# Two expert layers: the order of puts, picks and gate-and-up products in the block loop of a one-core transformer kernel

## The chip, the core and the metric

The kernel runs on one core of one Trainium2 chip. The core has a matrix engine (PE, or TensorE, with its weight loads shown apart as PEld), a vector engine (DVE), a scalar engine (ACT), a general engine (POOL), and a sync engine (SP) whose queue here issues nearly all DMA transfers. Each engine runs its own instruction list in order and waits on semaphores. The metric is the device time of one execution in microseconds. Before the change it is 2860.58 us, the median of 3 runs (2859.57 to 2863.24).

## The reference, cut to what matters

Two model blocks run one after the other on 256 tokens of width 1024. The second has two layers, each of which ends in a routed expert layer: a router picks 2 of 32 experts for each token, tokens are gathered by expert into blocks, and each block goes through its expert.

```python
def expert_block(args):
    x_blk, e = args
    hidden = jax.nn.silu(x_blk @ w_gate[e]) * (x_blk @ w_up[e])
    return hidden @ w_down[e]

yb = lax.map(expert_block, (xb, blk_e)).reshape(cap, d)
out = jnp.zeros((n_tok + 1, d), t.dtype).at[buf_tok].add(yb * buf_w[:, None].astype(yb.dtype))
```

Each expert has three float32 matrices, gate and up (1024 x 512) and down (512 x 1024), 2 MB each. So a layer reads 32 times 6 MB. The first expert layer has 512 tokens (the 256 and a context of 256), the second 256.

## The kernel before, in words

All work is written out by hand for each engine: `pe_program`, `act_program`, `dve_program`, `pool_program` and `sp_program` build one instruction list each, and semaphores tie them together. The order in a list is the order in the code. No planner moves anything.

An expert layer works in blocks of 32 token rows (`BL`). How many blocks an expert has is known only at run time, so for each of the 32 experts every engine has a loop `Fori(first_block(e), first_block(e + 1))` over the block number `g`. `first_block` (L2492) loads a register from memory, and each loop needs two. Since a block has only 32 rows, the matrix engine computes four column groups side by side (`q` in 0 to 3).

The steps of a block of the first expert layer (the "picked" layer, `pe_experts_picked`, L2741) are:

- **picks**: a 0/1 matrix times the token rows gathers the block's rows into PSUM (`pe_pick_rows`, L2736, 16 products, which the profile counts as 32 matmuls since float32 takes two passes). ACT copies them out (`xe`, L2793), PE transposes them (`pe_turn_picked`, L3232), and DVE copies them to `xeT` (L2803). DVE makes the pick matrix (`dve_places`, L2724 to L2730). Picks are done one block ahead: block `g` picks the rows of `g + 1`.
- **gate and up** products (L2761, 64 products, 128 matmuls) of `xeT` with the expert's first two matrices.
- **hidden**: ACT applies silu (L2791), DVE multiplies with the up half (L2821), PE transposes (L2768), DVE copies out (`hT`, L2824).
- **down** products (L2776, 16 products, 32 matmuls), copied out by ACT (L2796) and stored to memory by POOL (L2843).

In the code before, PE does gate and up of `g`, then the picks of `g + 1`, then the transpose of hidden, the transposes of the picked rows, and the down products. ACT does silu, then the copy of the picked rows, then the copy of the result.

The second expert layer (the "rows" layer, `pe_experts_rows`, L3245) differs at both ends. After the picks' transposes DVE applies gain and shift in two operations (`dve_turned`, L3352 and L3354). The result is not stored but added into PSUM by **puts** (`pe_put`, L3240): a transposed placement matrix `putT` times the block's result `yb`, in two halves around the picks. DVE makes `yb` (L3378), the pick matrix (`dve_picks`, L3322 to L3328) and the put matrix (`dve_puts`, L3337 to L3343) after the down products of each block, PE transposes the put matrix (L3276), and ACT copies it out (L3313). Puts are done one block late: block `g` puts the result of `g - 1`. The order on PE is gate and up, puts and picks, the transposes, and down.

The expert matrices come by SP's queue (L2361) into memory slots: nine in the picked layer, ten in the rows layer. When an expert's last block is done, a small matmul (L2779, L3291) signals `moe_ended`, and SP issues the transfers that reuse its slots. So the matrices of expert `e + 3` are asked for when expert `e` ends. In front of each expert's loop PE waits for the gate and up slots (L2753, L2754; L3256, L3257). The wait for the down slot is inside the loop.

Of the kernel before, what the change touches and what calls it, by code (L numbers as in the profile page):

```python
# [9 lines left out]
ACT = mybir.ActivationFunctionType  # L10
# [5 lines left out]
KT = D // P  # L16
# [2724 lines left out]
def pe_experts_picked(k, m):  # L2741
    pe, s, ps, l, BL, W, F = k.nc.tensor, k.s, k.ps, m.l, m.BL, m.W, m.F
    pe.wait_ge(*s["r_dve"].at(l, "based"))
    pe.wait_ge(*m.step("picks", 0, 2, 3))
    pe.wait_ge(*s["xs_out"].at(*HALVES[-1]))
    pe_pick_rows(k, m)
    pe.wait_ge(*m.step("x_out", 0, 1, 1))
    pe_turn_picked(k, m)
    for e in range(NE):
        sl = expert_slots(e)  # L2750
        wg, wu = (k.wslots[sl[i]].rearrange("p (k f) -> p k f", k=KT) for i in range(2))
        wd = k.wslots[sl[2]].rearrange("p (k f) -> p k f", k=4)
        pe.wait_ge(*s[f"slot{sl[0]}"].at("expert", l, e))  # L2753
        pe.wait_ge(*s[f"slot{sl[1]}"].at("expert", l, e))  # L2754
        with pe.Fori(first_block(k, m, e, ENG.PE), first_block(k, m, e + 1, ENG.PE)) as g:
            pe.wait_ge(*m.step("x_ready", g, 1, 1))
            pe.wait_ge(*m.step("hidden", g, 0, 1))
            for wv, a in ((wg, 0), (wu, F)):
                for t in range(KT):
                    for q in range(4):  # L2760
                        last = pe.matmul(ps[BL * q:BL * q + BL, 0, a:a + F], m.xeT[:, t, :], wv[:, t, F * q:F * q + F], start=(t == 0), stop=(t == KT - 1),  # L2761
                                         tile_position=(0, BL * q), skip_group_check=True)
            last.then_inc(m.n["gated"].sem, 1)
            pe.wait_ge(*m.step("picks", g, 5, 3))
            pe_pick_rows(k, m)
            pe.wait_ge(*m.step("hidden", g, 1, 1))
            pe.wait_ge(*m.step("h_ready", g, 0, 1))
            pe.transpose(ps[:, 2, 0:P], m.hb, k.c["ident"]).then_inc(m.n["h_turned"].sem, 1)  # L2768
            pe.wait_ge(*m.step("x_out", g, 2, 1))
            pe_turn_picked(k, m)  # L2770
            pe.wait_ge(*s[f"slot{sl[2]}"].at("expert", l, e))
            pe.wait_ge(*m.step("h_ready", g, 1, 1))
            pe.wait_ge(*m.step("y_ready", g, 0, 1))
            for f in range(4):
                for q in range(4):
                    last = pe.matmul(ps[BL * q:BL * q + BL, 3, 0:W], m.hT[:, f, :], wd[:, f, W * q:W * q + W], start=(f == 0), stop=(f == 3),  # L2776
                                     tile_position=(0, BL * q), skip_group_check=True)
            last.then_inc(m.n["down"].sem, 1)
        pe.matmul(ps[0:32, 0, 511:512], k.c["ident"][:, 0:32], k.c["ident"][:, 0:1], start=True, stop=True, skip_group_check=True).then_inc(*s["moe_ended"].up(l, "expert", e))  # L2779


def act_experts_picked(k, m):
    act, s, ps, l, BL, W = k.nc.scalar, k.s, k.ps, m.l, m.BL, m.W
    act.wait_ge(*s["r_dve"].at(l, "based"))
    act.wait_ge(*m.step("x_picked", 0, 1, 1))
    act.activation(m.xe, ps[:, 1, 0:256], ACT.Copy).then_inc(m.n["x_out"].sem, 1)
    for e in range(NE):
        with act.Fori(first_block(k, m, e, ENG.Activation), first_block(k, m, e + 1, ENG.Activation)) as g:
            act.wait_ge(*m.step("gated", g, 1, 1))
            act.wait_ge(*m.step("hidden", g, 0, 1))  # L2790
            act.activation(m.sil, ps[:, 0, 0:m.F], ACT.Silu).then_inc(m.n["silu"].sem, 1)  # L2791
            act.wait_ge(*m.step("x_picked", g, 2, 1))
            act.activation(m.xe, ps[:, 1, 0:256], ACT.Copy).then_inc(m.n["x_out"].sem, 1)  # L2793
            act.wait_ge(*m.step("down", g, 1, 1))
            act.wait_ge(*m.step("y_gone", g, 0, 1))
            act.activation(m.yring[:, bass.ds((g & 3) * W, W)], ps[:, 3, 0:W], ACT.Copy).then_inc(m.n["y_ready"].sem, 1)  # L2796
    act.activation(m.unread[:, 0:1], k.eps, ACT.Copy).then_inc(m.n["y_ready"].sem, 1)
# [447 lines left out]
def pe_experts_rows(k, m):  # L3245
    pe, s, ps, l, BL, W, F = k.nc.tensor, k.s, k.ps, m.l, m.BL, m.W, m.F
    pe.wait_ge(*s["r_dve"].at(l, "based"))
    pe.wait_ge(*m.step("picks", 0, 2, 3))
    pe_pick(k, m)
    pe.wait_ge(*m.step("x_out", 0, 1, 1))  # L3250
    pe_turn_picked(k, m)
    for e in range(NE):
        sl = row_slots(e)
        wg, wu = (k.wslots[sl[i]].rearrange("p (k f) -> p k f", k=KT) for i in range(2))
        wd = k.wslots[sl[2]].rearrange("p (k f) -> p k f", k=4)
        pe.wait_ge(*s[f"slot{sl[0]}"].at("expert", l, e))  # L3256
        pe.wait_ge(*s[f"slot{sl[1]}"].at("expert", l, e))  # L3257
        with pe.Fori(first_block(k, m, e, ENG.PE), first_block(k, m, e + 1, ENG.PE)) as g:
            pe.wait_ge(*m.step("x_ready", g, 2, 2))
            pe.wait_ge(*m.step("hidden", g, 0, 1))  # L3260
            for wv, a in ((wg, 0), (wu, F)):
                for t in range(KT):
                    for q in range(4):
                        last = pe.matmul(ps[BL * q:BL * q + BL, 0, a:a + F], m.xeT[:, t, :], wv[:, t, F * q:F * q + F], start=(t == 0), stop=(t == KT - 1),  # L3264
                                         tile_position=(0, BL * q), skip_group_check=True)
            last.then_inc(m.n["gated"].sem, 1)
            pe.wait_ge(*m.step("puts_out", g, 0, 1))
            pe.wait_ge(*m.step("y_ready", g, 0, 1))
            pe_put(k, m, 0).then_inc(m.n["half_put"].sem, 1)
            pe.wait_ge(*m.step("picks", g, 5, 3))  # L3270
            pe_pick(k, m)
            pe.wait_ge(*m.step("half_put", g, 1, 1))
            pe_put(k, m, 1)
            pe.wait_ge(*m.step("puts", g, 2, 3))
            for t in range(2):
                last = pe.transpose(ps[:, 3, 256 + t * P:256 + (t + 1) * P], m.put[:, t, :], k.c["ident"])  # L3276
            last.then_inc(m.n["puts_turned"].sem, 1)
            pe.wait_ge(*m.step("x_out", g, 2, 1))
            pe_turn_picked(k, m)
            pe.wait_ge(*m.step("hidden", g, 1, 1))  # L3280
            pe.wait_ge(*m.step("h_ready", g, 0, 1))
            pe.transpose(ps[:, 2, 0:P], m.hb, k.c["ident"]).then_inc(m.n["h_turned"].sem, 1)
            pe.wait_ge(*s[f"slot{sl[2]}"].at("expert", l, e))
            pe.wait_ge(*m.step("h_ready", g, 1, 1))
            pe.wait_ge(*m.step("puts_out", g, 1, 1))
            for f in range(4):
                for q in range(4):
                    last = pe.matmul(ps[BL * q:BL * q + BL, 3, 0:W], m.hT[:, f, :], wd[:, f, W * q:W * q + W], start=(f == 0), stop=(f == 3),  # L3288
                                     tile_position=(0, BL * q), skip_group_check=True)
            last.then_inc(m.n["down"].sem, 1)  # L3290
        pe.matmul(ps[0:32, 0, 511:512], k.c["ident"][:, 0:32], k.c["ident"][:, 0:1], start=True, stop=True, skip_group_check=True).then_inc(*s["moe_ended"].up(l, "expert", e))  # L3291
    total = first_block(k, m, NE, ENG.PE)
    pe.wait_ge(*m.step("puts_out", total, 0, 1))
    pe.wait_ge(*m.step("y_ready", total, 0, 1))
    pe_put(k, m, 0, stop=True).then_inc(m.n["half_put"].sem, 1)
    pe.wait_ge(*m.step("half_put", total, 1, 1))
    pe_put(k, m, 1, stop=True).then_inc(*s["acc_done"].up())


def act_experts_rows(k, m):  # L3300
# [3 lines left out]
    act.activation(m.xe, ps[:, 1, 0:256], ACT.Copy).then_inc(m.n["x_out"].sem, 1)  # L3304
    for e in range(NE):
        with act.Fori(first_block(k, m, e, ENG.Activation), first_block(k, m, e + 1, ENG.Activation)) as g:
            act.wait_ge(*m.step("gated", g, 1, 1))
            act.wait_ge(*m.step("hidden", g, 0, 1))
            act.activation(m.sil, ps[:, 0, 0:m.F], ACT.Silu).then_inc(m.n["silu"].sem, 1)  # L3309
            act.wait_ge(*m.step("x_picked", g, 2, 1))  # L3310
            act.activation(m.xe, ps[:, 1, 0:256], ACT.Copy).then_inc(m.n["x_out"].sem, 1)
            act.wait_ge(*m.step("puts_turned", g, 1, 1))
            act.activation(m.putT.rearrange("p t c -> p (t c)"), ps[:, 3, 256:512], ACT.Copy).then_inc(m.n["puts_out"].sem, 1)  # L3313


def dve_picks(k, m, g, wait=True):
# [309 lines left out]
```

## Time and profile before

| | |
|---|---|
| median of 3 runs | 2860.58 us |
| time of the profiled execution | 2861.28 us |
| its span, first to last instruction | 2860.1 us |
| busy: PE, PEld, DVE, ACT, POOL | 89%, 63%, 41%, 21%, 6% of the span |
| picked expert layer, first gate product to last down product | 1647.15 to 2132.8 us, 47 blocks |
| rows expert layer, the same | 2394.86 to 2850.0 us, 32 blocks |
| DMA read over the span | 670.09 MB |

The profile is of one execution. It lists, for each instruction, engine, start and duration, what the engine waited for before it, and the transfers with their landing. PEclk is the granted clock of the matrix engine as a share of full speed. A DMA share of 1 means that all 16 DMA engines were busy. "issue" is idle time of an engine for which no releasing instruction is seen. The chain of waits is followed back from the last instruction, each step to what released it. In it a transfer named there is one that some engine waited for.

### The profile page before, as it was taken

Reading aid. Unit: us, or ns where it says so; the run is one execution under the profiler, and the core shown is the slowest. Engines: PE = TensorE matmul, PEld = TensorE weight load, DVE = VectorE, ACT = ScalarE, POOL = GpSimd, SP = SyncE. Lnnn points to the kernel's source line nnn. Section 1 sums busy time; section 2 is a strip of 40 time slices with the busy share of each in tenths; the row PEclk is TensorE's granted clock in tenths of the full one; section 3 lists DMA queues with packets and bytes.
Section 4 is the critical chain, followed back from the end, with each engine's and each line's share of the span. In section 5 each row is a group of like instructions: output and inputs, shape, how many; then the busy total and the mean of one; then the engine's idle time right before and its main releaser. Section 6 shows DMA issues by size and latency. Waiting matters only on the chain.

```text
span 2860.1 us, 57236 instructions
## 1 busy us (share of the span) xinstructions
PE 2549.3 (89%) x23736; PEld 1804.0 (63%) x23736; DVE 1186.8 (41%) x2765; ACT 586.7 (21%) x1394; POOL 176.8 (6%) x346
## 2 busy tenths in 40 slices
PE   8999999998999999999998989887758997877776
PEld 7857778666857778668445566665546465554444
DVE  6563455646563465653138211111104253333323
ACT  3212322113212322122036211110102251000001
POOL 0001000010001000010000122221210000000000
PEclk9999999999999999999999999998978999999998
DMA  8844566456744566544210299999995126999997
GB/s 282 236 164 129 176 216 220 160 180 217 234 154 130 180 222 221 206 144 175 81 59 3 105 365 402 396 411 421 418 366 190 59 93 244 419 420 419 419 420 302
DMA packets 271389, 690.37 MB, mean 241 GB/s; under 512 B 35984, under 2 KB 163775, under 8 KB 254783
## 3 DMA queue, kind: packets, MB, share of 16 engines
q1 hardware_dynamic: 259904, 675.42, 63.1%
q0 software_dynamic: 7552, 10.76, 1.1%
q8 instruction: 168, 2.75, 0.4%
q10 hardware_dynamic: 3710, 0.99, 0.2%
q14 instruction: 55, 0.44, 0.0%
HBM read 670.09 MB, written 17.04 MB: 240 GB/s over the span
## 4 chain that ended last, share of the span: by engine, by line
PE 73%; DMA 14%; DVE 7%; issue 3%; ACT 2%; SPq 1%; ACTq 0%; POOL 0%; POOLq 0%; DVEq 0%
PE ps L756 18%; DMA arena<-in_moe_w_up 13%; PE ps L843 9%; PE ps L2761 5%; PE ps L1886 5%; PE ps L3264 3%; PE ps L2736 2%; PE ps L1945 2%; PE ps L2776 2%; PE ps L1251 2%; PE ps L2516 2%; PE ps L3225 1%; PE ps L3288 1%; PE ps L889 1%; PE ps L3070 1%
## 5 line engine op out<-in xcount | busy, mean ns | idle before, releaser
L756 PE MATMUL ps<-arena 128*128 128x256 f32 x2464 | 552.4, 381 | 9.9 <-DVE arena L1045 6.5
L756 PEld LDWEIGHTS ps<-arena 128*128 128x128 f32 x2464 | 460.6, 189 | 92.0 <-issue 13.0
L996 DVE TENSOR_TENSOR arena<-arena 128x1024 f32<-128x1024 f32 x176 | 214.8, 1223 | 143.4 <-PE ps L756 75.3
L843 PE MATMUL ps<-arena 128*128 128x512 f32 x616 | 266.1, 592 | 0.0
L2761 PE MATMUL ps<-arena 128*32 128x128 f32 x6016 | 196.4, 290 | 63.5 <-issue 61.0
L2761 PEld LDWEIGHTS ps<-arena 128*32 128x32 f32 x6016 | 180.6, 117 | 75.0 <-issue 69.7
L3264 PE MATMUL ps<-arena 128*32 128x128 f32 x4096 | 141.9, 298 | 80.0 <-issue 78.1
L843 PEld LDWEIGHTS ps<-arena 128*128 128x128 f32 x616 | 115.8, 189 | 144.4 <-issue 124.7
L3264 PEld LDWEIGHTS ps<-arena 128*32 128x32 f32 x4096 | 128.5, 120 | 85.3 <-issue 84.3
L2821 DVE TENSOR_TENSOR arena<-arena,ps 128x128 f32<-128x128 f32 x47 | 13.5, 288 | 313.7 <-ACT arena L2791 313.7
L1886 PE MATMUL ps<-arena 128*128 128x256 f32 (+2 forms) x384 | 133.4, 524 | 0.0
L2736 PE MATMUL ps<-arena 128*32 128x256 f32 x1536 | 101.1, 394 | 11.5 <-issue 8.4
L2843 POOL DMA_DIRECT2D expert_out<-arena x200 | 100.3, 502 | 69.3 <-issue 30.7
L1886 PEld LDWEIGHTS ps<-arena 128*128 128x128 f32 (+1 forms) x384 | 64.0, 172 | 62.8 <-issue 58.6
L3288 PE MATMUL ps<-arena 128*32 128x256 f32 x1024 | 62.1, 381 | 35.7 <-DVE arena L3376 35.7
L2776 PE MATMUL ps<-arena 128*32 128x256 f32 x1504 | 92.1, 381 | 0.4 <-issue 0.3
L920 ACT ACTIVATE arena<-ps 128x256 f32<-128x256 f32 x132 | 50.7, 384 | 147.7 <-PE ps L756 146.7
L2736 PEld LDWEIGHTS ps<-arena 128*32 128x32 f32 x1536 | 56.1, 112 | 37.2 <-issue 12.8
L1251 PE MATMUL ps<-arena 128*128 128x256 f32 x352 | 77.4, 379 | 0.0
L3309 ACT ACTIVATE arena<-ps 128x128 f32<-128x128 f32 x32 | 8.9, 278 | 318.7 <-PE ps L3264 318.7
L3225 PE MATMUL ps<-arena 128*32 128x256 f32 x528 | 69.6, 637 | 5.2 <-DVE arena L2480 3.3
L1251 PEld LDWEIGHTS ps<-arena 128*128 128x128 f32 x352 | 66.2, 189 | 9.5
(507 smaller groups left out, 3402.9 us busy)
## 6 DMA issues: line engine op xcount, KB each, us to landing
arena<-in_moe_w_gate SPq DMA_DIRECT2D x64, 2048.0 KB, 26.2
arena<-in_moe_w_up SPq DMA_DIRECT2D x64, 2048.0 KB, 26.2
arena<-in_moe_w_down SPq DMA_DIRECT2D x64, 2048.0 KB, 30.9
arena<-in_mod_w SPq DMA_DIRECT2D x24, 2048.0 KB, 13.9
arena<-in_w_gate SPq DMA_DIRECT2D x44, 1024.0 KB, 5.5
arena<-in_w_up SPq DMA_DIRECT2D x44, 1024.0 KB, 8.6
arena<-in_w_down SPq DMA_DIRECT2D x44, 1024.0 KB, 5.0
arena<-in_w_in SPq DMA_DIRECT2D x12, 1024.0 KB, 5.5
```

The source lines that it names most:

```text
L756: last = pe.matmul(out, tokens[j][:, t, :], weights[t], start=(t == 0 and j in ("P1", "P5", "P6", "P7")), stop=(t == HK - 1), skip_group_c ...
L843: pe.matmul(ps[:, DN_BANK[j], :], rows[j], w, start=(p == 0), stop=(p == CHUNKS - 1), skip_group_check=True).then_inc(*dn.up(l, f, p, j))
L996: V.tensor_tensor(out, a, b, op).then_inc(*s["w_sum"].up(l, f, c, i))
L1251: last = pe.matmul(dst, w[:, t, j * P:(j + 1) * P], src[:, t, :], start=(t == 0), stop=(t == KT - 1), skip_group_check=True)
L1886: last = pe.matmul(k.ps[o:o + m, j % 4, 0:ntok], w[:, t, c0:c0 + m], k.h2[:, t, 0:ntok], start=(t == 0), stop=(t == KT - 1), tile_position ...
L2736: last = k.nc.tensor.matmul(k.ps[32 * q:32 * q + 32, 1, 0:256], m.pick[:, t, :], m.rows[:, t, 256 * q:256 * q + 256], start=(t == 0), stop ...
L2761: last = pe.matmul(ps[BL * q:BL * q + BL, 0, a:a + F], m.xeT[:, t, :], wv[:, t, F * q:F * q + F], start=(t == 0), stop=(t == KT - 1), tile ...
L2776: last = pe.matmul(ps[BL * q:BL * q + BL, 3, 0:W], m.hT[:, f, :], wd[:, f, W * q:W * q + W], start=(f == 0), stop=(f == 3), tile_position= ...
L2843: k.nc.gpsimd.dma_start(k.ybuf[bass.ds(b * BL, BL), W * q:W * q + W], m.yring[BL * q:BL * q + BL, bass.ds((b & 3) * W, W)]).then_inc(which ...
L3225: last = k.nc.tensor.matmul(k.ps[32 * q:32 * q + 32, bank, 0:256], m.pick[:, t, :], rows, start=(t == 0), stop=(t == 1), tile_position=(0, ...
L3264: last = pe.matmul(ps[BL * q:BL * q + BL, 0, a:a + F], m.xeT[:, t, :], wv[:, t, F * q:F * q + F], start=(t == 0), stop=(t == KT - 1), tile ...
L3288: last = pe.matmul(ps[BL * q:BL * q + BL, 3, 0:W], m.hT[:, f, :], wd[:, f, W * q:W * q + W], start=(f == 0), stop=(f == 3), tile_position= ...
```

## The change

In both layers work that belongs to neighbouring blocks is moved to the front of the loop, ahead of the gate and up products. In the picked layer this is the picks of the next block. In the rows layer it is the two halves of the puts of the last block, the picks of the next, and the transposes of the put matrix. The waits for the gate and up slots move from in front of the loop into it, right before the products that need them. ACT's list follows: the copies of picked rows (and of the turned put matrix) come before silu. DVE, POOL and SP have the same lists as before.

```diff
@@ pe_experts_picked
-        pe.wait_ge(*s[f"slot{sl[0]}"].at("expert", l, e))
-        pe.wait_ge(*s[f"slot{sl[1]}"].at("expert", l, e))
         with pe.Fori(first_block(k, m, e, ENG.PE), first_block(k, m, e + 1, ENG.PE)) as g:
             pe.wait_ge(*m.step("x_ready", g, 1, 1))
+            pe.wait_ge(*m.step("picks", g, 5, 3))
+            pe_pick_rows(k, m)
+            pe.wait_ge(*s[f"slot{sl[0]}"].at("expert", l, e))
+            pe.wait_ge(*s[f"slot{sl[1]}"].at("expert", l, e))
             pe.wait_ge(*m.step("hidden", g, 0, 1))
...
             last.then_inc(m.n["gated"].sem, 1)
-            pe.wait_ge(*m.step("picks", g, 5, 3))
-            pe_pick_rows(k, m)
             pe.wait_ge(*m.step("hidden", g, 1, 1))
@@ act_experts_picked
+            act.wait_ge(*m.step("x_picked", g, 2, 1))
+            act.activation(m.xe, ps[:, 1, 0:256], ACT.Copy).then_inc(m.n["x_out"].sem, 1)
             act.wait_ge(*m.step("gated", g, 1, 1))
             act.wait_ge(*m.step("hidden", g, 0, 1))
             act.activation(m.sil, ps[:, 0, 0:m.F], ACT.Silu).then_inc(m.n["silu"].sem, 1)
-            act.wait_ge(*m.step("x_picked", g, 2, 1))
-            act.activation(m.xe, ps[:, 1, 0:256], ACT.Copy).then_inc(m.n["x_out"].sem, 1)
@@ pe_experts_rows
-        pe.wait_ge(*s[f"slot{sl[0]}"].at("expert", l, e))
-        pe.wait_ge(*s[f"slot{sl[1]}"].at("expert", l, e))
         with pe.Fori(first_block(k, m, e, ENG.PE), first_block(k, m, e + 1, ENG.PE)) as g:
-            pe.wait_ge(*m.step("x_ready", g, 2, 2))
-            pe.wait_ge(*m.step("hidden", g, 0, 1))
-            for wv, a in ((wg, 0), (wu, F)):
...
-            last.then_inc(m.n["gated"].sem, 1)
             pe.wait_ge(*m.step("puts_out", g, 0, 1))
             pe.wait_ge(*m.step("y_ready", g, 0, 1))
             pe_put(k, m, 0).then_inc(m.n["half_put"].sem, 1)
+            pe.wait_ge(*m.step("x_ready", g, 2, 2))
             pe.wait_ge(*m.step("picks", g, 5, 3))
             pe_pick(k, m)
             pe.wait_ge(*m.step("half_put", g, 1, 1))
...
             last.then_inc(m.n["puts_turned"].sem, 1)
+            pe.wait_ge(*s[f"slot{sl[0]}"].at("expert", l, e))
+            pe.wait_ge(*s[f"slot{sl[1]}"].at("expert", l, e))
+            pe.wait_ge(*m.step("hidden", g, 0, 1))
+            for wv, a in ((wg, 0), (wu, F)):
...
+            last.then_inc(m.n["gated"].sem, 1)
```

On PE, one expert of the picked layer reads in the order before as follows (L2495 are the register loads of `first_block`, L2761 gate and up, L2736 picks, L2768 the transpose of hidden, L3232 those of the picked rows, L2776 down):

```order
L2495 TENSOR_LOAD arena [waits slot0,slot5]
L2497 ISA
L2495 TENSOR_LOAD arena
L2497 ISA
L2755 UNCONDITIONAL_BRANCH
L2755 ISA
L2757 REGISTER_ALU [waits picked_x_ready]
L2761 MATMUL ps<-arena 32x128 [waits picked_hidden]
L2761 MATMUL ps<-arena 32x128 x63
L2764 ISA
L2736 MATMUL ps<-arena 32x256 [waits picked_picks]
L2736 MATMUL ps<-arena 32x256 x15
```

The same place after the change (here L2763 is gate and up):

```order
L2495 TENSOR_LOAD arena
L2497 ISA
L2753 UNCONDITIONAL_BRANCH
L2753 ISA
L2755 ISA [waits picked_x_ready]
L2736 MATMUL ps<-arena 32x256 [waits picked_picks]
L2736 MATMUL ps<-arena 32x256 x15
L2759 REGISTER_ALU [waits slot0,slot5]
L2763 MATMUL ps<-arena 32x128 [waits picked_hidden]
L2763 MATMUL ps<-arena 32x128 x63
L2768 MATMUL ps<-arena 128x128 [waits picked_h_ready,picked_hidden]
```

The slot wait has moved from the register loads to the gate products, and between the gate and up products and the transpose that waits for `hidden` nothing is left.

In the rows layer the list of PE after the change reads as follows (L3240 puts, L3225 picks, L3267 the transposes of the put matrix, L3275 gate and up, L3282 the transpose of hidden, L3288 down):

```order
L3240 MATMUL ps<-arena 128x256 [waits rows_y_ready,rows_puts_out]
...
L3225 MATMUL ps<-arena 32x256 [waits rows_picks]
...
L3240 MATMUL ps<-arena 128x256 [waits rows_half_put]
...
L3267 MATMUL ps<-arena 128x128 [waits rows_puts]
L3267 MATMUL ps<-arena 128x128
L3275 MATMUL ps<-arena 32x128 [waits rows_hidden,slot7,slot5]
L3275 MATMUL ps<-arena 32x128 x63
L3278 REGISTER_ALU
L3232 MATMUL ps<-arena 128x128 [waits rows_x_out]
L3232 MATMUL ps<-arena 128x128
L3282 MATMUL ps<-arena 128x128 [waits rows_h_ready,rows_hidden]
L3288 MATMUL ps<-arena 32x256 [waits rows_puts_out,rows_h_ready,slot9]
```

Before, the rows from L3240 to L3267 (then L3276) stood between the gate and up products and L3232. Now they stand ahead of the products, and the loop begins with the wait for `y_ready` of the block before.

## Rows read from the trace of the kernel before

**Rows 1.** Windows view, picked layer's first half: busy us per engine, PEclk, DMA share, GB/s

```profile
1660.00:1872.00 212.00, 191.97 (x4566) 140.72 (x4561) 40.82 (x143) 24.45 (x71) 50.36 (x115) 0.98 0.99 400
```

**Rows 2.** Windows view, same columns, rows layer from 2520 us

```profile
2520.00:2838.00 318.00, 226.02 (x4185) 152.82 (x4180) 94.32 (x364) 21.97 (x63) 0.00 (x0) 0.93 1.01 416
```

**Rows 3.** Chain of waits, where it leaves PE in the picked layer: start, us, what

```profile
1907.74 25.16 DMA arena<-in_moe_w_up
```

**Rows 4.** Timeline of SP's queue: issues of expert 15's down, expert 16's gate

```profile
1855.46 0.43 SPq L2361 DMA_DIRECT2D arena<-in_moe_w_down  x1
1871.86 0.34 SPq L2361 DMA_DIRECT2D arena<-in_moe_w_gate  x1
```

**Rows 5.** DMA view of these two issues: count, KB, us from issue to landing

```profile
arena<-in_moe_w_down SPq DMA_DIRECT2D x1, 2048.0 KB, 18.5
...
arena<-in_moe_w_gate SPq DMA_DIRECT2D x1, 2048.0 KB, 9.0
```

**Rows 6.** Timeline, a block of the picked layer from its picks on: start, us, engine

```profile
1849.77 1.95 PE L2736 MATMUL ps<-arena 128*32 128x256 f32 x32
1850.10 0.28 ACT L2791 ACTIVATE arena<-ps 128x128 f32<-128x128 f32 x1 [3.02 <-PE ps L2761]
1850.50 0.29 DVE L2821 TENSOR_TENSOR arena<-arena,ps 128x128 f32<-128x128 f32 x1 [4.71 <-ACT arena L2791]
...
1851.65 0.33 PE L2768 MATMUL ps<-arena 128*128 128x128 f32 x1
...
1852.02 0.29 DVE L2824 COPY arena<-ps 128x128 f32<-128x128 f32 x1 [1.23 <-PE ps L2768]
...
1852.19 0.44 PE L3232 MATMUL ps<-arena 128*128 128x128 f32 x2 [0.21 <-ACT arena L2793]
...
1852.56 1.93 PE L2776 MATMUL ps<-arena 128*32 128x256 f32 x32
```

**Rows 7.** Lines view of PE, 1647 to 1872 us: busy, mean ns, idle before

```profile
L2768 PE MATMUL ps<-arena 128*128 128x128 f32 x25 | 8.3, 334 | 0.0
```

**Rows 8.** Waits view of PE, the same stretch: total us, times, longest

```profile
PE ps L2761 <- issue: 9.0, 7, 2.9
...
PE ps L2736 <- issue: 4.4, 3, 2.0
```

**Rows 9.** Timeline, one block of the rows layer, from down products to down products

```profile
2467.04 1.94 PE L3288 MATMUL ps<-arena 128*32 128x256 f32 x32 [1.11 <-DVE arena L3376]
...
2469.03 0.42 DVE L3378 TENSOR_TENSOR arena<-ps,arena 128x256 f32<-128x256 f32 x1 [2.09 <-PE ps L3288]
...
2469.10 3.70 PE L3264 MATMUL ps<-arena 128*32 128x128 f32 x128
...
2470.32 0.23 DVE L3327 TENSOR_TENSOR arena<-arena 128x64 f32<-128x64 f32 x1
...
2472.73 0.71 PE L3240 MATMUL ps<-arena 32*128 32x256 f32 x8
...
2473.34 0.29 DVE L3372 TENSOR_TENSOR arena<-arena,ps 128x128 f32<-128x128 f32 x1 [1.15 <-ACT arena L3309]
...
2473.38 2.03 PE L3225 MATMUL ps<-arena 128*32 128x256 f32 x16
...
2476.26 0.38 PE L3232 MATMUL ps<-arena 128*128 128x128 f32 x2
...
2476.68 0.42 DVE L3352 TENSOR_TENSOR arena<-ps,arena 128x256 f32<-128x256 f32 x1 [3.05 <-PE ps L3232]
...
2477.86 1.94 PE L3288 MATMUL ps<-arena 128*32 128x256 f32 x32 [1.11 <-DVE arena L3376]
```

**Rows 10.** Chain of waits, last expert of each layer, from its weights' landing

```profile
2120.34 1.42 issue
2121.76 6.46 PE ps L2761 x128
...
2837.88 1.31 issue
2839.20 3.75 PE ps L3264 x128
```

More of the change, by code:

```diff
@@ L3255, in pe_experts_rows @@
         wd = k.wslots[sl[2]].rearrange("p (k f) -> p k f", k=4)
-        pe.wait_ge(*s[f"slot{sl[0]}"].at("expert", l, e))
-        pe.wait_ge(*s[f"slot{sl[1]}"].at("expert", l, e))
         with pe.Fori(first_block(k, m, e, ENG.PE), first_block(k, m, e + 1, ENG.PE)) as g:
-            pe.wait_ge(*m.step("x_ready", g, 2, 2))
-            pe.wait_ge(*m.step("hidden", g, 0, 1))
-            for wv, a in ((wg, 0), (wu, F)):
[L3262 to L3265, printed above, removed]
-            last.then_inc(m.n["gated"].sem, 1)
             pe.wait_ge(*m.step("puts_out", g, 0, 1))
@@ L3277, in pe_experts_rows @@
             last.then_inc(m.n["puts_turned"].sem, 1)
+            pe.wait_ge(*s[f"slot{sl[0]}"].at("expert", l, e))
+            pe.wait_ge(*s[f"slot{sl[1]}"].at("expert", l, e))
+            pe.wait_ge(*m.step("hidden", g, 0, 1))
+            for wv, a in ((wg, 0), (wu, F)):
+                for t in range(KT):
+                    for q in range(4):
+                        last = pe.matmul(ps[BL * q:BL * q + BL, 0, a:a + F], m.xeT[:, t, :], wv[:, t, F * q:F * q + F], start=(t == 0), stop=(t == KT - 1),
+                                         tile_position=(0, BL * q), skip_group_check=True)
+            last.then_inc(m.n["gated"].sem, 1)
             pe.wait_ge(*m.step("x_out", g, 2, 1))
@@ L3306, in act_experts_rows @@
         with act.Fori(first_block(k, m, e, ENG.Activation), first_block(k, m, e + 1, ENG.Activation)) as g:
-            act.wait_ge(*m.step("gated", g, 1, 1))
-            act.wait_ge(*m.step("hidden", g, 0, 1))
-            act.activation(m.sil, ps[:, 0, 0:m.F], ACT.Silu).then_inc(m.n["silu"].sem, 1)
             act.wait_ge(*m.step("x_picked", g, 2, 1))
@@ L3313, in act_experts_rows @@
             act.activation(m.putT.rearrange("p t c -> p (t c)"), ps[:, 3, 256:512], ACT.Copy).then_inc(m.n["puts_out"].sem, 1)
+            act.wait_ge(*m.step("gated", g, 1, 1))
+            act.wait_ge(*m.step("hidden", g, 0, 1))
+            act.activation(m.sil, ps[:, 0, 0:m.F], ACT.Silu).then_inc(m.n["silu"].sem, 1)
 def dve_picks(k, m, g, wait=True):
```

## The prediction, made before the changed kernel ran

> **What bounds the kernel now.** I read the windows first, then the chain of waits, then SP's issues with their landings, then the timeline of single blocks. The windows alone would mislead. From 1660 to 1872 us the picked layer shows a DMA share of 0.99 at 400 GB/s beside 191.97 us of PE work in 212 [rows 1], so both look full. The chain decides: it stays on PE from the first block until it leaves for a weight transfer at 1907.74 us [rows 3]. From there to the end of the layer PE waits for weights. The rows layer is the same with a short PE part. From 2520 us on the share is 1.01 at 416 GB/s and PE has 226.02 us of work in 318 [rows 2].
>
> Then I ask whether the transfers run free of PE in the first part. They do not. Expert 15's down matrix, issued at 1855.46, lands 18.5 us later, at 1874.0. Expert 16's gate matrix is issued at 1871.86, when expert 13 ends, and lands 9.0 us later, at 1880.9 [rows 4, 5]. That is 6.9 us after the transfer ahead of it, although 2.1 MB take 5.0 us at 416 GB/s [rows 2]. So the queue ran dry by 1.9 us: only 2.1 us of work was left in it at the issue. Each microsecond by which PE ends expert 13 later is a microsecond by which this matrix lands later, and from about here on the transfers are the bound with no slack to give it back. PE's block time in the first part sets the end of the layer.
>
> **The picked layer, per block.** Call E the start of the picks, when the gate and up products have been handed over: 1849.77. Before, the down products start at 1852.56, E + 2.79 [rows 6]. Under the picks lie silu (E + 0.33) and the multiplication (E + 0.73 to E + 1.02), so hidden is ready long before the picks end, and that wait is free. In the new order nothing covers it. PE idles from E to about E + 1.10, transposes hidden, and the copy starts 0.37 us after the transpose as now (1851.65 to 1852.02): E + 1.47 to E + 1.76. With 0.1 for the release, down starts at E + 1.86. The two transposes of the picked rows (0.44) fit behind hidden's, since their copy by ACT was done under the gate products. The picks still cost PE's time, now in front. They take 1.88 from their start to the next transpose [rows 6]; in front of narrower products I take 1.8. So a block costs 1.8 + 1.86 = 3.66 where it cost 2.79: **+0.87 us**. The pick matrix doesn't hold this up, since DVE has made it during the down products.
>
> 25 blocks are done by the end of expert 13 [rows 7]: 25 x 0.87 = 21.8. The first block must also wait for its successor's pick matrix, made after `x_ready`: +0.6, an estimate from two short DVE operations. Together 22.4.
>
> Something may give way. In this stretch PE stood 9.0 + 4.4 = 13.4 us in ten spells called "issue", inside rows of matmuls that wait for no one [rows 8]. I read these as instruction supply that comes late. If the new idle time falls between the request and the stall, the supply catches up, by at most 0.87 a spell: 8.7 in all. Bounds are 0 (the idle time falls elsewhere) and 13.4 (all go). The nearest reading is half of 8.7: **-4.4**.
>
> The Trainium skill (Runtime: NRT & Kernel Launch, section Instruction fetch mechanics) says that the next page of instructions is fetched while the current one runs and that the cost of a page boundary is mostly hidden. The spells in the trace, 13.4 us, do not fit "mostly hidden". By the page there would be nothing to win back, and the layer would pay the whole 22.4.
>
> **The picked layer's tail.** For the last expert, time runs from the landing of its up matrix. After the landing come 1.42 us of issue [rows 10]. The register loads of the loop stand behind the slot wait before and ahead of it after, so I take 1.3 of it as saved. From E on the tail is 2.79 - 1.86 = 0.9 shorter. **-2.2.** This holds only at the end. The same saving at each earlier expert hastens nothing, since the transfers don't wait for it there.
>
> **The rows layer, per block.** With S the start of the down products (2467.04), a block takes 10.82 to the next (2477.86). Gate and up take 3.63 of it (2469.10 to 2472.73) and 5.13 lie from their end to the down products [rows 9]. After the change, counted from S: `yb` is made from 1.99 to 2.41 and the first put starts at 2.46. It takes 0.65. The pick matrix is written at 3.28 to 3.51, so the picks start at 3.56. Picks, second put and the transposes of puts take 2.88 (2473.38 to 2476.26), to 6.44. Gate and up end at 10.07. Then silu and the multiplication, whose start is 0.61 after E (2473.34 against 2472.73) and whose end is at 0.90. DVE next applies gain and shift, which I let start at E + 0.87, and from that start to the down products it is 1.18 (2476.68 to 2477.86): E + 2.05. Sum 12.12: **+1.3 us** a block.
>
> All 32 experts have one block here, and from 2520 us on transfers need 15.1 us an expert (6.29 MB at 416 GB/s) [rows 2]. 12.1 plus a spell of issue stays under it. So only the first two experts' delay reaches the transfers, about 0.9 (the first block has no `yb` to wait for) and 1.3: **+2.2**, bounds 0 and 4. The tail gains 1.2 of the 1.31 of issue [rows 10] and 5.13 - 2.05 = 3.1, **-4.3**. It would be less (1.5 less) if the last gate products ran at the slow clock, as those of the picked layer do (6.46 for 128 against 3.75) [rows 10].
>
> **The sum.** 22.4 - 4.4 - 2.2 + 2.2 - 4.3 = +13.7. The profiled execution took 2861.28, so 2875.0. It lies 0.7 above the median, and on the median the forecast is **2874.3 us**. What is not in it: DVE, POOL and SP keep their order, and ACT has much idle time (24.45 us of work in 212) [rows 1].
>
> **Rivals.** *The transfers hide it all.* If the queue never really ran dry, the 22.4 and 2.2 fall away and the tails remain: -6.5, 2854 us, faster. For it speaks the share of 0.99 [rows 1]. Against it the landing 6.9 us behind the last one, and 400 GB/s where 416 are to be had. It would need over 20 us of queued work at the release of expert 13, and there were 2.1. Chance 0.07.
>
> *The late instruction supply takes up the idle time.* All 13.4 us go: 22.4 - 13.4 - 2.2 + 2.2 - 4.3 = +4.7, 2865 us, about the size that can't be told from none. For it speaks that the spells are there at all; against it that one spell of 2.9 is longer than the 0.87 a block adds [rows 8]. Chance 0.10.
>
> *The clock.* An idle stretch of 1.1 us in each block, then 0.2, is new in the picked layer. If the granted clock fell to its 1.2 GHz level in part of the blocks, gate and up would cost 6.46 instead of about 3.6 in each [rows 10], with 25 blocks up to +70; in a quarter of them +18, 2892 us. Against it: rows-layer blocks now wait 1.11 us each ahead of their down products, and gate and up after them still take 3.70 [rows 9]. Chance 0.08. The Trainium skill (TensorE: Matmul & The Clock Gate, section A second HAM failure mode: psum-queue depth-cycling) tells of a kernel whose short idle times between groups made the clock oscillate. It speaks against this change, but the granted 0.98 of [rows 1] is with idle times too, if shorter ones. By that rule it would be this rival's 2892 and by the row the forecast.
>
> *The rows layer becomes PE-bound too*, with long issue spells or slow gate products on top of 12.1, past the 15.1 from which it decides. At half a microsecond over in 27 experts, +14, 2888 us. Chance 0.05.
>
> **Numbers.** The forecast has 0.70. 0.2% of this time is 5.7 us, which is about what a measurement can tell from no change. Faster: 0.07 for hidden transfers and 0.01 from the rest, 0.08. Within: most of the second rival, 0.08. Slower: 0.84. The range goes from the second rival, 2864, to beyond the forecast with nothing won back (2879) and part of the clock's case, 2886.
>
> **What would show it.** In the profile after: the gap from the end of gate and up to down in the picked layer is 1.9 and not 2.8, with 1.1 of idle before L2768 released by DVE. Blocks cycle in 8.9 us instead of 8.0. The chain leaves PE for a transfer some 18 us later than 1907.74, or later still. The landing of a gate matrix in the first part stays about 9 us after its issue. No issue spell follows the last weights. The rows layer keeps its length within 3 us. Wrong would be: the picked layer no longer than before (then the transfers were the bound), or gate and up of 5 us and more in its first part (then it was the clock).

## The result, and the profile after

The changed kernel took 2875.91 us, the median of 6 runs (2872.21 to 2881.22), against 2861.98 before in the same session (6 runs). The ratio is 1.0049, with a 95% interval of 1.0037 to 1.0061: about 14 us slower, which is past the 0.2% that can be told from no change. Forecast were 2874.3 us and slower. A second timing in another session gave 1.0047 (1.0030 to 1.0064). The ratio should be carried on and not the times, since the kernel before gave medians of 2864 to 2866 us in the later sessions.

The windows of the profile after, the answer to [rows 1, 2] (busy us per engine, PEclk, DMA share, GB/s):

```profile
1660.00:1890.00 230.00, 194.25 (x4788) 152.54 (x4781) 39.51 (x144) 25.46 (x73) 54.32 (x124) 0.99 0.94 375
2535.00:2850.00 315.00, 228.59 (x4221) 150.79 (x4221) 92.33 (x362) 21.91 (x63) 0.00 (x0) 0.96 1.01 419
```

In the first part of the picked layer the transfers now move 375 GB/s and not 400, at a share of 0.94 and not 0.99. The clock has not fallen. The rows layer is as full as it was. The DMA engines have lost time in one place, and it is the one where PE sets the pace.

The chain of waits leaves PE for a transfer here, where [rows 3] had 1907.74:

```profile
1959.65 35.04 DMA arena<-in_moe_w_up
```

It is 52 us later, more than the delay of the layer. The transfer named here was issued when expert 19 ended, the one before when expert 16 ended (1907.07), so the chain leaves PE three experts later. It isn't PE's first wait for weights: it had already stood 3.19 us for expert 20's up matrix, until 1964.25, which the chain does not pass.

SP's issue of expert 16's gate matrix and its landing, which answer to [rows 4, 5]:

```profile
1886.22 0.34 SPq L2361 DMA_DIRECT2D arena<-in_moe_w_gate  x1
```

```profile
arena<-in_moe_w_gate SPq DMA_DIRECT2D x1, 2048.0 KB, 8.9
```

From issue to landing it took 8.9 us, as before 9.0, so the queue ran dry again and the delay of the issue (14.4 us, of which 1.8 arose ahead of the layer) went straight into the landing.

A block of the picked layer, from its gate and up products on, the answer to [rows 6]. L2763 is gate and up, L2793 silu:

```profile
1870.08 3.68 PE L2763 MATMUL ps<-arena 128*32 128x128 f32 x128
...
1873.91 0.28 ACT L2793 ACTIVATE arena<-ps 128x128 f32<-128x128 f32 x1 [3.19 <-PE ps L2763]
1874.30 0.29 DVE L2821 TENSOR_TENSOR arena<-arena,ps 128x128 f32<-128x128 f32 x1 [6.86 <-ACT arena L2793]
...
1874.65 0.33 PE L2768 MATMUL ps<-arena 128*128 128x128 f32 x1 [0.88 <-DVE arena L2821]
...
1875.01 0.29 DVE L2824 COPY arena<-ps 128x128 f32<-128x128 f32 x1 [0.42 <-PE ps L2768]
...
1875.41 1.93 PE L2776 MATMUL ps<-arena 128*32 128x256 f32 x32 [0.21 <-issue]
...
1877.13 1.94 PE L2736 MATMUL ps<-arena 128*32 128x256 f32 x32
```

(The profile counts two matmuls for each float32 product, here x128 for 64; no run shows why.) The brackets show the new idle time: 0.88 us before the transpose of hidden, ended by the multiplication on DVE, and 0.21 before the down products. From these down products to the next it is 8.79 us (1875.41 to 1884.20), where it was 8.03. That holds inside an expert. Where the expert changes, an unhindered interval was 8.36 us and is now 8.97.

PE's waits from 1647 to 1895 us, the answer to [rows 8]:

```profile
PE ps L2768 <- DVE arena L2821: 21.9, 25, 0.9
PE ps L2763 <- issue: 10.3, 5, 3.1
PE ps L2776 <- issue: 5.8, 25, 0.7
...
PE ps L2736 <- issue: 0.8, 1, 0.8
```

25 blocks waited 21.9 us for the multiplication. The view ends 9 us after expert 13, and one spell of 2.3 us (at 1891.3) belongs to expert 14. Up to expert 13's end (1885.92) the spells of late instructions are 5 with 8.8 us (8.0 and 0.8), where there were 10 with 13.4. The 5.8 of L2776 is mostly the 0.21 of each block.

One block of the rows layer, the answer to [rows 9]. L3275 is gate and up, L3267 the transposes of the put matrix:

```profile
2486.09 1.94 PE L3288 MATMUL ps<-arena 128*32 128x256 f32 x32 [0.71 <-issue]
...
2488.65 0.71 PE L3240 MATMUL ps<-arena 32*128 32x256 f32 x8 [0.63 <-DVE arena L3378]
...
2489.65 2.03 PE L3225 MATMUL ps<-arena 128*32 128x256 f32 x16 [0.28 <-DVE arena L3327]
...
2492.62 3.71 PE L3275 MATMUL ps<-arena 128*32 128x128 f32 x128
...
2497.22 0.33 PE L3282 MATMUL ps<-arena 128*128 128x128 f32 x1 [0.52 <-DVE arena L3372]
```

The three waits forecast are there: for `yb`, for the pick matrix and for hidden. The first put starts 2.56 after the down products (forecast 2.46), the picks 3.56 (3.56), gate and up 6.53 (6.44). The block takes 12.17 us (2486.09 to the next down products at 2498.26), with 12.12 forecast.

Both tails, the answer to [rows 10], in the chain of waits:

```profile
2135.09 0.23 issue
2135.32 4.93 PE ps L2763 x112
2140.26 1.08 issue
...
2143.77 3.18 PE ps L2776 x32
```

```profile
2853.47 2.62 issue
2856.09 5.40 PE ps L3275 x128
...
2863.38 1.97 PE ps L3288 x32
```

Of the 1.42 us after the last landing 0.23 are left. But the down products at the picked layer's end take 3.18 us and not 1.91, and the gate products at the rows layer's end 5.40 and not 3.75: both ran in part at the 1.2 GHz level (granted clock 0.61 and 0.68 over them), the second after 2.62 us of idle PE.

### The profile page after: what moved, and what is told of

Read it like the earlier page. It is cut to its first block, busy times and chain, and to the rows that moved or that the text cites. A ratio compares the mean times of both kernels' runs of the same rounds, so it can differ in the third digit from the quotient of the medians.

```text
span 2875.5 us, 57251 instructions
## 1 busy us (share of the span) xinstructions
PE 2552.6 (89%) x23736; PEld 1812.6 (63%) x23736; DVE 1181.4 (41%) x2765; ACT 586.3 (20%) x1394; POOL 176.8 (6%) x346
## 4 chain that ended last, share of the span: by engine, by line
PE 73%; DMA 13%; DVE 7%; issue 3%; ACT 2%; SPq 2%; ACTq 0%; POOL 0%; DVEq 0%; POOLq 0%
PE ps L756 18%; PE ps L843 9%; DMA arena<-in_moe_w_down 7%; PE ps L2763 5%; PE ps L1886 5%; DMA arena<-in_moe_w_up 4%; PE ps L2776 3%; PE ps L1945 2%; PE ps L2736 2%; PE ps L1251 2%; PE ps L3275 2%; PE ps L2516 2%; SPq L2361 2%; PE ps L3288 1%; PE ps L889 1%
## 5 line engine op out<-in xcount | busy, mean ns | idle before, releaser
L756 PEld LDWEIGHTS ps<-arena 128*128 128x128 f32 x2464 | 462.3, 190 | 92.4 <-issue 13.0
L2763 PE MATMUL ps<-arena 128*32 128x128 f32 x6016 | 193.5, 287 | 46.8 <-DMA arena<-in_moe_w_up 28.1
L2763 PEld LDWEIGHTS ps<-arena 128*32 128x32 f32 x6016 | 181.8, 115 | 60.7 <-issue 54.1
L843 PEld LDWEIGHTS ps<-arena 128*128 128x128 f32 x616 | 115.8, 189 | 144.4 <-issue 124.7
L2821 DVE TENSOR_TENSOR arena<-arena,ps 128x128 f32<-128x128 f32 x47 | 13.6, 288 | 395.8 <-ACT arena L2793 395.8
L3275 PE MATMUL ps<-arena 128*32 128x128 f32 x4096 | 134.8, 293 | 44.7 <-issue 44.7
L3275 PEld LDWEIGHTS ps<-arena 128*32 128x32 f32 x4096 | 125.6, 118 | 51.9 <-issue 51.8
L3372 DVE TENSOR_TENSOR arena<-arena,ps 128x128 f32<-128x128 f32 x32 | 9.2, 288 | 242.8 <-ACT arena L3313 242.8
L2776 PE MATMUL ps<-arena 128*32 128x256 f32 x1504 | 97.6, 395 | 10.4 <-issue 10.2
L2736 PE MATMUL ps<-arena 128*32 128x256 f32 x1536 | 95.4, 387 | 6.0 <-DVE arena L2730 3.0
L3288 PE MATMUL ps<-arena 128*32 128x256 f32 x1024 | 62.7, 381 | 23.2 <-issue 16.1
L2776 PEld LDWEIGHTS ps<-arena 128*32 128x32 f32 x1504 | 54.4, 112 | 41.6 <-issue 24.8
L3225 PE MATMUL ps<-arena 128*32 128x256 f32 x528 | 67.0, 637 | 12.0 <-DVE arena L3327 8.6
L2736 PEld LDWEIGHTS ps<-arena 128*32 128x32 f32 x1536 | 51.8, 111 | 33.9 <-issue 5.3
```

The source lines that it names most:

```text
L756: last = pe.matmul(out, tokens[j][:, t, :], weights[t], start=(t == 0 and j in ("P1", "P5", "P6", "P7")), stop=(t == HK - 1), skip_group_c ...
L843: pe.matmul(ps[:, DN_BANK[j], :], rows[j], w, start=(p == 0), stop=(p == CHUNKS - 1), skip_group_check=True).then_inc(*dn.up(l, f, p, j))
L2736: last = k.nc.tensor.matmul(k.ps[32 * q:32 * q + 32, 1, 0:256], m.pick[:, t, :], m.rows[:, t, 256 * q:256 * q + 256], start=(t == 0), stop ...
L3225: last = k.nc.tensor.matmul(k.ps[32 * q:32 * q + 32, bank, 0:256], m.pick[:, t, :], rows, start=(t == 0), stop=(t == 1), tile_position=(0, ...
```

## The experiments

A ratio is the time of the kernel named over that of the kernel before in the same session, with its 95% interval; differences in us are worked out from it. Besides the ratios I compare stage lengths, read alike from every profile. The picked layer is counted from its first transposes of picked rows (L3232) to the end marker of expert 13, and to that of expert 31. The rows layer runs from its own first such transposes to its last end marker, and the middle part lies between the two layers.

| order of picked / rows layer | picked, to expert 13 | picked, whole | middle | rows |
|---|---|---|---|---|
| old / old (before) | 226.0 | 487.0 | 260.5 | 456.7 |
| old / new (rows change alone) | 222.8 | 484.2 | 262.0 | 454.4 |
| old / old (waits moved alone) | 225.8 | 485.0 | 264.7 | 457.0 |
| new / new (after, first profile) | 238.6 | 499.4 | 263.9 | 454.5 |
| new / new (second profile) | 242.9 | 501.9 | 264.9 | 453.0 |
| new / old (picked change alone) | 242.8 | 501.8 | 267.1 | 455.7 |
| new up to expert 16 / old | 239.7 | 500.7 | 262.4 | 457.8 |
| new from expert 17 on / old | 226.6 | 485.7 | 261.9 | 456.1 |
| new from expert 17 on / new | 225.1 | 484.8 | 263.6 | 452.5 |
| half of the picks in front / old | 225.2 | 485.5 | 263.3 | 456.2 |
| half of the picks in front / new | 226.3 | 487.0 | 262.1 | 452.5 |
| new, idle time filled / old | 250.7 | 512.0 | 263.7 | 457.8 |

### The picked layer's change alone

```diff
 (pe_experts_picked and act_experts_picked as after, pe_experts_rows and act_experts_rows as before)
```

> The change in the picked layer alone, the rows layer as before. My theory (PE sets the pace up to about expert 16, and a block pays the uncovered wait for hidden): blocks of the first half cycle in 8.8 us against 8.03, the layer ends 10 to 13 us later, the whole is 11 to 13 us slower than before. Rival, the transfers set the pace and the loss came from elsewhere in the program: 0 to 3 us slower. Rival, the rows layer's moved puts cost too: then this one is under 9 us slower and the rows change alone makes up the rest.

Measured: 1.0042 (1.0028 to 1.0056), 12.0 us slower at a median of 2865.75 before. Unhindered blocks cycle in 8.79 us. The loss is in the picked layer, 501.8 us long.

### The rows layer's change alone

```diff
 (pe_experts_rows and act_experts_rows as after, pe_experts_picked and act_experts_picked as before)
```

> The change in the rows layer alone, the picked layer as before. My theory: a block costs 1.3 us more (12.17 us against 10.82), the transfers hide it from the third expert on, and the last expert is 3 to 4 us shorter: 0 to 3 us faster than before. Rival, the layer is bound by PE too: 10 us and more slower. Its picked layer is a second sample of the old order: blocks of 8.03 us, and the spells of late instructions should sum to about 13 us up to expert 13 if they belong to the order, and to something else if they vary from program to program.

Measured: 0.9982 (0.9973 to 0.9991), 5.2 us faster, more than the 0 to 3 expected. Its blocks cycle in 12.16 us, and the layer is 2.3 us shorter. Some of the rest may be the picked layer, which has the old order and took 2.8 us less than in the profile of before. So one profile of each kernel is not enough for a difference of 3 us in a stage. The spells up to expert 13 sum to 12.6 us, near the 13 expected if they belong to the order. The rival (bound by PE too) falls.

### The slot waits moved, nothing else

```diff
-        pe.wait_ge(*s[f"slot{sl[0]}"].at("expert", l, e))
-        pe.wait_ge(*s[f"slot{sl[1]}"].at("expert", l, e))
         with pe.Fori(first_block(k, m, e, ENG.PE), first_block(k, m, e + 1, ENG.PE)) as g:
             pe.wait_ge(*m.step("x_ready", g, 1, 1))
+            pe.wait_ge(*s[f"slot{sl[0]}"].at("expert", l, e))
+            pe.wait_ge(*s[f"slot{sl[1]}"].at("expert", l, e))
             pe.wait_ge(*m.step("hidden", g, 0, 1))
```

(in both layers)

> Both layers in the order before, only the waits for the gate and up slots moved into the loop, behind the register loads. My theory: the 1.3 to 1.4 us of issue after the last landing go, once in each layer, all else is the same: 2 to 3 us faster than before. Rival, the spell after the landing is the semaphore's own latency and not the register loads: no change.

Measured: 0.9988 (0.9979 to 0.9997), 3.4 us faster. The end of its chain of waits:

```profile
2841.52 0.23 issue
2841.75 5.37 PE ps L3264 x128
```

The 1.31 us after the landing are down to 0.23, so they were the register loads and the start of the loop, which stood behind the wait, and not the semaphore. In this profile the gate products behind them ran in part at the 1.2 GHz level (granted clock 0.68, 5.37 us against 3.75), which takes more back than the 1.1 won. But so they did in five of the other six profiles with the rows layer's old order; the kernel before, with 3.75, is the exception. Against those five, where 13.3 to 13.5 us lie from the landing of the last up matrix to the end marker, this one took 12.4: the 1.1 us are there. What a single profile shows of the tail hangs on the clock as much as on the order.

### Half of the picks in front, half behind

```diff
             pe.wait_ge(*m.step("x_ready", g, 1, 1))
+            pe.wait_ge(*m.step("picks", g, 5, 3))
+            pe_pick_rows(k, m, (0, 1))
+            pe.wait_ge(*s[f"slot{sl[0]}"].at("expert", l, e))
+            pe.wait_ge(*s[f"slot{sl[1]}"].at("expert", l, e))
             pe.wait_ge(*m.step("hidden", g, 0, 1))
...
             last.then_inc(m.n["gated"].sem, 1)
-            pe.wait_ge(*m.step("picks", g, 5, 3))
-            pe_pick_rows(k, m)
+            pe_pick_rows(k, m, (2, 3))
             pe.wait_ge(*m.step("hidden", g, 1, 1))
```

> The picked layer with half of the picks (8 of 16 products) in front of the gate and up products and half behind them, slot waits in the loop, the rows layer as before. My theory, that the price is the uncovered wait for hidden: about 0.9 us of work behind the products covers most of it, the copy of the picked rows then sets the down products, a block takes 8.0 to 8.2 us, and with the shorter tail the whole lies between 2 us faster and 4 us slower than before. Rival, that anything put between a block's down products and the next gate products costs its own time there (0.9 us a block for half, 1.8 for all): half of what the full move costs, 6 us slower.

Measured: 0.9997 (0.9986 to 1.0009), no difference from before. PE and the multiplication in one of its blocks (L2764 is gate and up, L2778 down):

```profile
1863.59 1.05 PE L2736 MATMUL ps<-arena 128*32 128x256 f32 x16
...
1864.45 3.68 PE L2764 MATMUL ps<-arena 128*32 128x128 f32 x128
...
1867.94 1.05 PE L2736 MATMUL ps<-arena 128*32 128x256 f32 x16
...
1868.67 0.29 DVE L2823 TENSOR_TENSOR arena<-arena,ps 128x128 f32<-128x128 f32 x1 [5.56 <-ACT arena L2793]
...
1869.86 1.93 PE L2778 MATMUL ps<-arena 128*32 128x256 f32 x32
```

From down products to down products it is 8.03 us (1861.83 to 1869.86), to the hundredth the old order's block. 16 matmuls behind the gate products cover the wait as well as 32. The rival, a cost for whatever is put in front, falls.

### The new order only for the first 17 experts, or only for the rest

```diff
+        early = e < 17        # in the other kernel: e >= 17; where it is false, the old order
...
+            if early:
+                pe.wait_ge(*m.step("picks", g, 5, 3))
+                pe_pick_rows(k, m)
...
+            if not early:
+                pe.wait_ge(*m.step("picks", g, 5, 3))
+                pe_pick_rows(k, m)
```

(ACT's list follows for the same experts, the rows layer is as before)

> The new order of the picked layer for experts 0 to 16 alone, the old one for 17 to 31, rows layer as before. My theory (the price is paid while PE sets the pace, nothing is paid or won in the middle, and the last expert wins 1 to 2 us): 12 to 15 us slower than before, the whole price of the picked layer's change. Rival, the price falls on every block alike, 47 of them: 7 to 9 us slower.

> The new order of the picked layer for experts 17 to 31 alone, rows layer as before. My theory: the transfers hide the longer blocks and the last expert is shorter by about 2 us: 1 to 3 us faster than before. Rival, the price falls on every block alike: 3 to 5 us slower.

The changed kernel ran again beside these:

> The changed kernel again, beside the next three on one chip. Its first timing gave 14 us over before, its two halves alone 12.0 over and 5.2 under, which sum to 7. Additive halves: 5 to 9 us slower. Halves that hinder each other: 12 to 16 us slower.

Measured: new for experts 0 to 16, 1.0053 (1.0037 to 1.0068), 15 us slower. New for 17 to 31, 0.9991 (0.9981 to 1.0001), 2.6 us faster with an interval that just holds no change. The whole change again, 1.0047 (1.0030 to 1.0064), 13.5 us slower. The price is paid where PE sets the pace, and nowhere else. The last of the three also lies in the range that stood for halves that hinder each other (12 to 16), not in the one for halves that add up (5 to 9); more on this below.

The second profile of the changed kernel also shows what the rows layer's tail runs into when its gate products are fast:

```profile
2829.01 35.08 DMA arena<-in_moe_w_down
...
2864.78 1.97 PE ps L3288 x32
```

The down products wait there for the landing of the down matrix, the last transfer of all, so little of the tail is left to win.

### Idle time filled

```diff
             last.then_inc(m.n["gated"].sem, 1)
+            for t in range(4):
+                for q in range(4):
+                    pe.matmul(ps[BL * q:BL * q + BL, 2, 256:256 + F], m.xeT[:, t, :], k.c["ident"][:, 0:F], start=(t == 0), stop=(t == 3),
+                              tile_position=(0, BL * q), skip_group_check=True)
```

(on top of the picked layer's change alone)

> The picked layer's change alone, with 16 more products (32 matmuls, about 0.9 us, results unused) in each block between the gate and up products and the transpose of hidden. My theory, that PE idles there for silu and the multiplication: they run in idle time, blocks stay at 8.8 to 8.9 us, and the whole is where the picked layer's change alone is, plus 0 to 5 us for 15% more instructions to supply. Rival, that the longer block comes from PE's own work (slower or reordered products): 0.9 us more for each of 25 blocks, 20 us above that.

Measured: 1.0086 (1.0070 to 1.0102). One of its blocks (L2768 the added products, L2772 the transpose of hidden, L2780 down) and its waits:

```profile
1869.28 3.70 PE L2763 MATMUL ps<-arena 128*32 128x128 f32 x128
1872.77 1.08 PE L2768 MATMUL ps<-arena 128*32 128x128 f32 x32
1873.85 0.33 PE L2772 MATMUL ps<-arena 128*128 128x128 f32 x1
...
1874.61 0.64 PE L2780 MATMUL ps<-arena 128*32 128x256 f32 x8 [0.21 <-issue]
```

```profile
PE ps L2763 <- issue: 8.7, 4, 2.6
...
PE ps L2768 <- issue: 5.7, 3, 2.5
```

1.08 us of added work leave the block at 8.79 us (1865.82 to 1874.61): the idle time was free. Still the kernel is 12.6 us over the picked layer's change alone (0.44% of 2866), and I had expected 0 to 5. With the intervals of both ratios the excess lies between about 7 and 19 us. The picked layer took 512.0 us against 501.8, and 250.7 against 242.8 to expert 13. The picked change alone waited 7.1 + 0.9 us for instructions in 5 spells over this stretch. Here it is 8.7 and 5.7 in these two rows and more at the down products. So more instructions in the loop cost time even where their execution is free. That the shortage is of instruction supply is my reading of "issue" inside unbroken rows of matmuls. The DMA view has a queue that it calls "instruction", with transfers of 16 KB. Here it is for the kernel before, from 1660 to 1872 us:

```profile
q8 instruction: 21, 0.34, 0.6%
```

With the added products it is 24 from 1660 us to the end of expert 13, with the picked layer's change alone 21. That agrees with the reading. But no run changed the supply by itself.

### Two versions from the findings

```diff
 (picked layer: the order by expert as above with e >= 17; rows layer as after)
```

> A version made from the findings: the new order of the picked layer for experts 17 to 31 alone, and the rows layer's change whole. If each part keeps what it gave alone (2.6 and 5.2 us): 6 to 9 us faster than before. If the halves hinder each other as the sum of the first runs hinted: 2 to 4 us faster.

```diff
 (picked layer: half of the picks in front, half behind; rows layer as after)
```

> The second candidate: half of the picks in front and half behind in the picked layer, and the rows layer's change whole. Parts alone gave 0.9 and 5.2 us: 5 to 7 us faster than before if they add up. Its middle part between the layers is a further sample of how much that part differs from program to program.

Measured: 0.9985 (0.9974 to 0.9996), 4.3 us faster, and 0.9992 (0.9983 to 1.0001), 2.3 us faster with an interval that just holds no change. Both gave less than the sum of their parts (6 to 9 and 5 to 7 us had been expected), and neither beats the rows change alone (0.9982), though the intervals overlap. The first is clear of both the kernel before and the one after.

## Why the prediction was right

Forecast 2874.3, slower; measured 2875.9. The mechanism was right. That the sum came within 2 us is in part luck, since several terms were off by 1 to 3 us and made up for each other. In its order:

- **PE sets the pace of the picked layer's first part.** Right. The landing 9 us after the issue stayed, the transfers lost rate, and the same edit to experts 17 and later costs nothing.
- **+0.87 us a block.** It was 0.76 inside an expert (8.79 against 8.03). The chain from silu to down was as forecast, 1.83 us against 1.86; the picks in front cost a little less than the 1.8 taken. 25 x 0.76 = 19.0 where 21.8 stood. And where the expert changes it was only 0.61 (8.97 against 8.36). The forecast let the wait's new place win at the last expert alone. While PE sets the pace it seems to win about 0.15 us at each of 13 changes too, 2 us in all.
- **The first block, +0.6.** It was 0.3. From the transposes of its picked rows to the down products it took 7.9 us before and 9.0 now, 1.1 more, of which 0.76 is the price of any block.
- **Late instructions give 4.4 back.** The spells themselves did. Up to expert 13 they sum to 12.1 to 13.9 us in the five profiles of the table whose order there is old in full (mean 12.9), and to 8.0 to 10.0 in the four where it is new in full, filled idle time left out (mean 8.7): 4.2 less. But some spells are followed by matmuls at the 1.2 GHz level, and with the new order more of them were. All that the first 24 block intervals took above unhindered ones (8.03 and 8.36, or 8.79 and 8.97) is 17.5 us in the mean of the old and 16.3 in that of the new, with 19.4 in the profile of before and 14.6 in the first one after. So the net gain is about 1 us and not 4.4. Whether the spells shrank by the new idle time, as the forecast had it, or because the code lies differently, no run separates. The rival in which all is given back falls.
- **The delay at expert 13's end, 18.0.** Over the same profiles the old order takes 225.3 us to there (mean of five) and the new 241.0 (mean of four): 15.7.
- **The whole picked layer, +15.8.** Over the kernels with one order throughout it takes 485.4 and 501.0 us (three profiles each, one of the old ones with the waits moved): +15.6. The single pair of profiles, 487.0 and 499.4, shows 12.4 and would have had me look for a gain that isn't there. The parts don't add up as well as the whole: 15.7 to expert 13 and -1.7 in the tail give 14.0.
- **The picked tail, -2.2.** From the landing of the last up matrix to the end marker it takes 12.1 us in the mean of the three profiles with the old tail, and 10.4 in that of the five with the new: -1.7. In the single pair the way to the down products went from 10.6 to 8.7 us, with a spell of 1.08 in it, and the slow down products took 1.3 back. The term held in the main.
- **The rows layer, +2.2 and -4.3.** Together -2.1 forecast. The mean is 456.8 us over seven profiles with the old order there and 453.4 over five with the new: -3.4. The early delay, read as the time from the layer's start to the landing of its last up matrix, is 443.7 and 445.3 in these means: +1.6 where 2.2 stood. The tail from there to the end marker is 13.1 and 8.1: -5.0. It depends on the clock of the last gate products. Where they ran at the full level it was 11.9 us (old, one profile) and 7.4 (new, three), where they ran in part at the low one 12.4 to 13.5 (old, six; without the moved waits 13.3 to 13.5) and 9.1 (new, two). At either level the new order gains 4.2 to 4.4, the 4.3 of the forecast. The pair of before and first after compares a tail of the full level with one of the low level, so it shows -2.7 in the tail, and -2.2 for the layer (456.7 and 454.5).
- **The rivals.** Hidden transfers: refuted by the new order for the first 17 experts alone, at 15 us. The clock: 0.99 in the stretch, where [rows 1] has 0.98, so refuted as a general price. But over the same stretch (from 1660 to 1890 us) the granted clock is 0.97 in the second profile and 0.96 with the picked layer's change alone, so it takes a part that differs from profile to profile, and it showed at both tails. The rows layer bound by PE: refuted.

The sum by stage means is 15.6 - 3.4 = 12.2, the measured difference 13.5 to 14. Two things stay open. The middle part, which no edit touches, took 260.5 to 267.1 us, and the shortest is that of the kernel before. Its mean is 262.6 us over the seven profiles whose picked layer begins in an order that is old or half old, and 264.4 over the five with the new, which would fill the gap. Within that spread it isn't shown that the change causes it. And the halves alone sum to 6.8 us (12.0 - 5.2), with intervals of about 4 and 3 us on the two, against 13.5 and 14 for the whole. The two combined versions also fell short of the sum of their parts, which hints at an interaction or at placement of code, and nothing here decides which.

## What to carry to other kernels

Work that stands between a product and the step that waits for its result may be cover. Moving it out of the way of a wait for weights gains at the last expert of a stretch that waits for weights, where nothing later takes the gain up, and costs the uncovered latency in every block where the engine sets the pace. Ask which of the two bounds each part of the loop: a DMA share of 0.99 did not mean that transfers set the pace, and the landing time of a transfer issued late did. Half of the cover was enough here, so the move need not be all or nothing. And where a term is smaller than the difference between two profiles of one kernel (up to 4 us in a stage here), take it from several, and compare stretches that ran at the same clock.

## What the runs showed of the hardware that I had not expected

Matmuls whose execution was free (1.08 us in an idle gap, the block unchanged at 8.79 us) made the kernel 12.6 us slower, with more and longer spells of "issue" in rows of matmuls. The Trainium skill, Runtime: NRT & Kernel Launch, section Instruction fetch mechanics, has the cost of page boundaries mostly hidden. In this loop, beside transfers at 360 to 400 GB/s, the spells came to 8 to 14 us up to expert 13 (225 to 245 us) with either order, if they are that cost. The same section says that a taken branch to a page that isn't held stalls the fetch. The kernel has a run-time loop for each expert, and no run here tells the two apart.

The spells come at the same blocks from program to program. In all five profiles of the old order the 4th, 7th, 11th and 20th block of the picked layer start their down products 2 us or more later than an unhindered block would. In none of the four of the new order is the 11th late by more than 0.6 us. With the idle time filled it is again, by 2.9.

The level at which the rows layer's last gate products ran went with the idle time of PE just before them, though not without exception. After 0.23, 0.79 and 0.97 us the 128 matmuls took 3.70 us, all at full clock. After 2.4 to 4.1 us they took 5.2 to 5.4 in eight profiles, in part at the 1.2 GHz level. In the ninth, the kernel before, they took 3.75 after 2.76 us.
